# A two-layer model's MLPs: seven block products for the up matrix alone, or for the down matrix too

## What is computed

```python
        hn = rmsnorm(x, p['norm_mlp'][layer])
        u = jnp.maximum(hn @ p['w_up'][layer], 0)
        x = x + (u * u) @ p['w_down'][layer]
```

## Time and profile before

| what | value |
|---|---|
| median of 3 runs | 3455.08 us |
| lowest and highest | 3453.11 and 3457.73 us |
| span of the profiled execution (the page gives no other time for it) | 3458.2 us |
| PE busy | 3249.8 us, 94% |
| DVE, ACT, POOL busy | 1632.3, 1045.6, 1291.6 us |
| matmuls | 22572, of them 11568 at L2229 in the two MLPs |
| DMA | 205.13 MB, mean 59 GB/s |

### The profile page before, as it was taken

One profiled execution on the slowest core, in us unless ns is written; L12 is line 12 of the kernel. 1 busy time (PEld: TensorE's weight loads), 2 busy tenths in 40 slices (PEclk: granted clock), 3 DMA queues, 4 the chain that ended last, 5 costly groups with the idle time before them and its releaser, 6 DMA issues. The chain is left out here.

```text
span 3458.2 us, 54690 instructions
## 1 busy us (share of the span) xinstructions
PE 3249.8 (94%) x22572; PEld 3033.5 (88%) x22572; DVE 1632.3 (47%) x2715; ACT 1045.6 (30%) x1940; POOL 1291.6 (37%) x878
## 2 busy tenths in 40 slices
PE   7999988899999999999998898999889999999998
PEld 7999867889999999997887587788669999999998
DVE  5961157626544445541012254565564744455443
ACT  5310145324332232341001233233232422223334
POOL 4433224444644444454321121111124544444453
PEclk9999989999999999999999898999899999999999
DMA  4111323231111111123232322000231111111111
GB/s 146 43 38 56 102 26 73 47 104 44 43 50 43 38 50 50 50 70 130 78 102 72 89 44 59 9 6 8 93 137 42 45 44 37 50 50 50 50 38 71
DMA packets 257881, 205.13 MB, mean 59 GB/s; under 512 B 66053, under 2 KB 222207, under 8 KB 257220
## 3 DMA queue, kind: packets, MB, share of 16 engines
q1 hardware_dynamic: 252108, 201.21, 19.9%
q10 hardware_dynamic: 5528, 0.45, 0.1%
HBM read 159.42 MB, written 33.40 MB: 56 GB/s over the span
## 5 line engine op out<-in xcount | busy, mean ns | idle before, releaser
L2229 PE MATMUL ps<-u_r,wslots_r 128*128 128x272 f32 x5784 | 747.5, 289 | 9.3 <-DVE u_r L2565 3.0
L2229 PEld LDWEIGHTS ps<-u_r,wslots_r 128*128 128x128 f32 x5784 | 735.7, 189 | 14.7 <-DVE u_r L2565 6.1
L2229 PE MATMUL ps<-low_r,wslots_r 128*128 128x272 f32 x3312 | 579.3, 289 | 5.1 <-ACT low_r L2392 3.2
L2229 PEld LDWEIGHTS ps<-low_r,wslots_r 128*128 128x128 f32 x3312 | 479.2, 189 | 7.3 <-ACT low_r L2392 4.3
L2229 PE MATMUL ps<-hn_r,wslots_r 128*128 128x272 f32 x2472 | 476.3, 291 | 4.7 <-DVE hn_r L2565 3.0
L2575 DVE TENSOR_TENSOR xT<-xT,ps 128x544 f32<-128x544 f32 x480 | 338.4, 718 | 285.6 <-PE ps L2229 285.5
L2229 PEld LDWEIGHTS ps<-hn_r,wslots_r 128*128 128x128 f32 x2472 | 375.7, 190 | 8.1 <-DVE hn_r L2565 6.1
L2486 POOL TENSOR_TENSOR wslots<-rawm 128x512 f32<-128x512 f32 x150 | 197.6, 1318 | 379.4 <-PE ps L2229 367.6
L1777 PE MATMUL ps<-hn_r,wslots_r 128*128 128x364 f32 (+1 forms) x1392 | 274.6, 330 | 11.0 <-DVE Z L1990 4.9
L2491 POOL TENSOR_TENSOR wslots_r<-rawd,wslots_r 128x512 fp32r<-128x512 f32 x128 | 169.5, 1335 | 278.4 <-ACT wslots_r L2375 278.4
L1777 PEld LDWEIGHTS ps<-hn_r,wslots_r 128*128 128x128 f32 x1392 | 236.3, 189 | 17.5 <-DVE Z L1990 7.6
(11 more groups left out here) (705 smaller groups left out, 5662.2 us busy)
## 6 DMA issues: line engine op xcount, KB each, us to landing
rawm<-in_w_up SPq DMA_DIRECT2D x63, 512.0 KB, 4.7
rawd<-in_w_down SPq DMA_DIRECT2D x112, 256.0 KB, 2.8
raw<-in_w_in_even SPq DMA_DIRECT2D x28, 512.0 KB
xT<-x_saved SPq DMA_DIRECT2D x2, 4368.0 KB, 15.6
more_r<-more_r SPq DMA_DIRECT2D x28, 256.0 KB, 3.4
xT<-in_cache_fox_kv SPq DMA_DIRECT2D x12, 512.0 KB, 4.0
x_saved<-Z SPq DMA_DIRECT2D x1, 4368.0 KB, 14.8
Z<-in_x_prompt SPq DMA_DIRECT2D x8, 512.0 KB, 4.7
```

The source lines that it names most:

```text
L2229: m = pe.matmul(acc(i)[:, c], r32(w), r32(moved[:, qw * c:qw * (c + 1)]), start=start, stop=stop, skip_group_check=True)
```

## The change

`mlp_fourteen` replaces `mlp_seven`. It has two phases with seven block products in each.

**Upward.** Group 0 is plain as before; sets 1 to 15 are the seven products "1563724" of a group. The variant used has only 4 weight sums (`s1` to `s4`, two of them in place) and nests its results: a product accumulates onto the PSUM bank of an earlier one, once ACT has copied that (`first`) or DVE has added it (`more`). After the ReLU and the square, DVE makes four differences of the four hidden blocks (`differences`, `last_difference`), and SP stores all seven, squares and differences, as float32 to DRAM (`hid`).

**Downward.** 16 further sets, two for each 512 rows of `w_down`, again seven products "1563724" of 24 matmuls each (two output tiles x 12). The operand of a product is loaded back from DRAM over the place of the input block that is no longer needed, a pair of tiles at a time, rounded by ACT (`operand_high`) and reduced by DVE (`operand_low`). DVE adds each bank to the residual after each product (`added`), 14 times per set. The same four weight sums are made by POOL.

**Queues.** `raw` and a new `rawn` hold two sets of raw weights, loaded in four DMAs of 256 KB. SP's order per upward set is: weights of the set after next, then the seven stores. The final tiles of the residual come at eight points in the last two sets (`closes`) instead of one by one. Group 0's down product, which stood between the plain products and group 1, is gone from there.

The core of the diff:

```diff
-def mlp_seven(pr, I, layer, ps, W, wslots, rawd, xT, x, u, row, gx, norm, ending, saved=None):
+def mlp_fourteen(pr, I, layer, ps, W, wslots, rawn, hid, xT, x, u, row, gx, norm, ending, saved=None):
...
+    order, slot_of = "1563724", (0, 2, 1, 3)
+    top = G - 1
+    jobs = [(s, m) for s in range(1, 2 * G) for m in order]
...
+    closes = {(14, "3"): down[0:2], (14, "7"): down[2:4], (14, "2"): down[4:6], (14, "4"): down[6:8],
+              (15, "7"): down[8:12], (15, "2"): down[12:14], (15, "4"): down[14:16]}
+    adds_to = {"1": (0, 0), "5": (4, 1), "6": (0, 1), "3": (0, 1), "7": (4, 1), "2": (0, 0), "4": (4, 0)}
...
+    def turns(j):
+        s, x = 1 + j // 7, j % 7
+        y = j - 7 * (G - 2) - 3
+        found = [(0, order[y])] if 0 <= y < 7 else []
+        for q in range(1, Q):
+            y = j - 7 * (G - 1 + 2 * (q - 1)) - 6
+            if 0 <= y < 7:
+                found.append((q, order[y]))
+        return found
+    stores = [f"st_{n}" for n in ("h11", "h12", "h22", "h21", "t1", "t2", "t4")]
...
+            for s in range(1, top):
+                need(pool_, ("low", (s, "4")))
+                load_weights(s + 2)
+                for m in "3156724":
+                    store(s, m)
...
+            def up(s, m):
+                need(pool_, ("low", (s, m)))
+                if m == "1":
+                    need(dve_, ("hidden", s - 2, "h21") if s > 1 else ("hidden", 0, "h11"))
+                elif m == "5":
+                    need(dve_, ("more", s - 1, "h12") if s > 1 else ("hidden", 0, "h12"))
+                elif m == "2":
+                    need(dve_, ("more", s - 1, "h11") if s > 1 else ("hidden", 0, "h22"))
+                elif m in "637":
+                    need(act_, ("first", s, {"6": "h11", "3": "h22", "7": "h12"}[m]))
...
+            def room(d, m, i):
+                if m == "1":
+                    return ("added", d - 1, "2", i) if d else (("hidden", top - 1, "h21"), ("more", top, "h12"))[i]
+                if m == "5":
+                    return ("added", d - 1, "4", i) if d else (("more", top, "h11"), ("hidden", top, "h21"))[i]
+                return ("added", d, {"6": "1", "3": "5", "7": "6", "2": "3", "4": "7"}[m], i)
...
+            def first(s, m):
+                name = {"1": "h11", "5": "h22", "6": "h12"}[m]
+                need(pe_, ("M", s, m))
+                sem, value = parked_sem(name, s - 1)
+                act.wait_ge(s_[sem], value)
+                need(dve_, ("t3", s - 1))
+                step(("first", s, name), A.activation(two(park(name, s)), acc(up_acc(s, m)), ACT.Copy))
...
+            for j, (s, m) in enumerate(jobs):
+                if s < G and m in "156":
+                    first(s, m)
+                if j + 4 < len(jobs):
+                    high_of(jobs[j + 4])
+                if s < G and m in "3724":
+                    square(s, {"3": "h12", "7": "h22", "2": "h11", "4": "h21"}[m])
+                for q, mm in turns(j):
+                    operand_high(q, mm)
...
+            for s, m in jobs:
+                if m == "1":
+                    s1(s)
+                if m == "5":
+                    s3(s)
+                    s2(s)
+                if m == "6":
+                    s4(s)
+                low_of((s, m))
...
+            def differences(g):
+                need(act_, ("square", g, "h12"))
+                need(act_, ("square", g, "h11"))
+                parked_free("t1", g)
+                step(("t1", g), V.tensor_tensor(park("t1", g), park("h12", g), park("h11", g), ALU.subtract))
+                need(act_, ("square", g, "h22"))
+                need(dve_, ("t1", g))
+                parked_free("t2", g)
+                step(("t2", g), V.tensor_tensor(park("t2", g), park("h22", g), park("t1", g), ALU.subtract))
+                step(("t3", g), V.tensor_tensor(park("h12", g), park("h12", g), park("h22", g), ALU.subtract))
...
+            waiting = []
+            for j, (s, m) in enumerate(jobs):
+                d = s - G
+                if s < G:
+                    if m in "372":
+                        more(s, m)
+                    if m == "2":
+                        differences(s)
+                    if m == "4":
+                        need(pe_, ("M", s, "4"))
+                        parked_free("h21", s)
+                        need(dve_, ("t4", s - 1))
+                        hidden(s, "h21", acc(up_acc(s, "4")))
+                        last_difference(s)
+                else:
+                    added(d, m, 0)
+                    added(d, m, 1)
+                for q, mm in turns(j):
+                    operand_low(q, mm)
+                for n, t in waiting:
+                    lower(n, t)
+                waiting = closes.get((d, m), []) if low is not None else []
```

More of the change, by code:

```diff
@@ L2230, in product, with plain @@
                 return m
-            X = (XH, XL)
[L2232 to L2237, removed]
+            for i in range(NC + 1):
+                m = pe.matmul(sums[0:width[i], i:i + 1], norm["total"][:, P * i:P * i + width[i]], W["ones"][:, 0:1], start=True, stop=True)
+            done(m, "sums")
+            def plain(k, t):
+                return slice(TP * k + hw * t, TP * k + hw * t + hw)
+            X = (XH, XL)
             wa, wb = (wslots[:, 0], wslots[:, 2]), (wslots[:, 1], wslots[:, 3])
@@ L2387, in unit @@
[L2387 to L2399 removed]
+                step(("high", job), A.activation(r32(slot(job, 0)), source(job), ACT.Copy))
@@ L2460, in _ @@
-            for n, t in down:
-                c = slice(hw * t, hw * t + hw)
-                if (n, t) in ((2, 1), (4, 1)):
-                    high_of(("D", last - 1, 1 + n // 2))
-                    high_of(("D", last, 1 + n // 2))
-                need(dve_, ("add", G - 1, n, t))
-                step(("squared", n, t), A.activation((squares(n) if n else total)[:, c], xT[:, n, c], ACT.Square))
-                step(("scaled", n, t), A.activation(r32(high[:, n, c]) if rounded is not False else high[:, n, c], xT[:, n, c], ACT.Copy, scale=gcols[:, n:n + 1]))
+            high_of(jobs[0])
@@ new lines, in _ @@
+            for k in range(4):
+                x_high("6", k)
+            high_of(jobs[1])
+            square(0, "h12")
+            square(0, "h11")
+            for m in "47":
+                for k in range(4):
+                    x_high(m, k)
+            square(0, "h22")
+            high_of(jobs[2])
+            high_of(jobs[3])
+            square(0, "h21")
+            for j, (s, m) in enumerate(jobs):
[7 more added lines that the diff above has]
+                    operand_high(q, mm)
+                for n, t in closes.get((s - G, m), []):
+                    c = slice(hw * t, hw * t + hw)
+                    if n in (2, 3) and t:
+                        need(pe_, ("N", 15, "7", 1))
+                    need(dve_, ("final", n, t))
+                    step(("squared", n, t), A.activation((squares(n) if n else total)[:, c], xT[:, n, c], ACT.Square))
+                    step(("scaled", n, t), A.activation(r32(high[:, n, c]) if rounded is not False else high[:, n, c], xT[:, n, c], ACT.Copy, scale=gcols[:, n:n + 1]))
@@ new lines, in x_low, with hidden @@
+            def x_low(m, k):
+                hi, lo = operand(m, k)
+                need(act_, ("x_high", m, k))
+                if m == "6":
+                    need(dve_, ("x", "7", k))
+                    need(dve_, ("x", "4", k))
+                step(("x_low", m, k), V.tensor_tensor(r32(lo), lo, r32(hi), ALU.subtract))
+            def hidden(g, name, src):
+                t = 1 if name in ("h12", "h22") else 0
+                step(("hidden", g, name), V.scalar_tensor_tensor(out=two(park(name, g)), in0=src, scalar=0.0, in1=two(norm["row"][:, hw * t:hw * t + hw]),
+                                                                 op0=ALU.max, op1=ALU.mult))
@@ new lines, in more, with parked_free @@
+            def more(s, m):
+                name = {"3": "h12", "7": "h22", "2": "h11"}[m]
+                need(pe_, ("M", s, m))
+                need(act_, ("first", s, name))
+                t = two(park(name, s))
+                step(("more", s, name), V.tensor_tensor(t, t, acc(up_acc(s, m)), ALU.add))
+                need(dve_, ("more", s, name))
+                hidden(s, name, t)
+            def parked_free(name, g):
+                if g:
+                    sem, value = parked_sem(name, g - 1)
+                    dve.wait_ge(s_[sem], value)
@@ L2682, in _ @@
-            for y, (n, t) in enumerate(down):
-                add(G - 1, n, t)
-                if low is not None and y >= 1:
-                    lower(*down[y - 1])
-            if low is not None:
-                lower(*down[-1])
+                x_sum("4", k)
+            need(pe_, ("plain", 1, 1))
+            for k in range(4):
+                x_sum("7", k)
+            hidden(0, "h22", acc(2))
+            for k in range(4):
+                x_low("6", k)
```

(1 more changed line is left out.)

626 lines of the change are left out of this document (240 added, 386 removed).

## The result

The changed kernel takes 3513.84 us, the median of four runs (3512.21 to 3519.5), against 3454.61 for the kernel before in the same comparison: a ratio of 1.0169, interval 1.0155 to 1.0184, some 59 us slower. 3535 was forecast.

The account below looks back on a forecast made before the run. The prediction took the MLP to be bound by PE's rate. Savings of 48.5 us a layer against added waits, start, end and clock gave +40 a layer, +80 in both: 3455 + 80 = 3535 us, range 3392 to 3590.

Parts of the forecast that it names:

- 384 matmuls fewer: Downward part of each layer's MLP falls from 3072 to 2688 matmuls at 0.1264 us each: 48.5 us less a layer.
- waits at "6": Upward set borders: PE waits at product "6" for ACT's copy of "1", 14 times 2.4 us, 34 a layer, bounds 0 to 41.
- first downward set: Border from upward to downward phase: operand rounding and low parts delay PE by 6.1 + 2.5, 9 us a layer, bounds 3 to 12.
- downward pairs: Borders of downward sets: PE waits behind operand low parts and adds, 7 pairs x 2.3 = 16 us a layer, bounds 0 to 20.
- start: Start of each MLP: PE at 867 instead of 850.7, 16 less the 4.8 lost today: 11 us a layer, bounds 5 to 16.
- end: End of each MLP: POOL's 14 additions of squares finish later after PE, costing 7.5 and 6 us, together 13, bounds 0 to 20.
- clock, beyond the start: Half clock after PE's waits loses 1.7 us after one of two, 0.85 for each of 14: 12 us a layer, bounds 0 to 24.
- The chain: Upward borders: sums, squares and differences queue on POOL, ACT and DVE, so PE restarts near 15.0 instead of 12.1: 2.9 or 1.8 us.
- rival (2): Faster: DVE's three differences run without POOL between, so upward waits and clock loss vanish; 3405, or 3384 with downward waits hidden; chance 0.29.
- The turn: DVE and POOL, both waiting, alternate in 0.59 + 1.16 = 1.75 us, not the 2.01 of two whole instructions.
- rival (4): Each turn holds the other engine a whole instruction, 2.01 us; "6" waits 4.2; 3609, or 3585 without the clock; chance 0.08.
- DMAs: Seven stores per set and the operand loads on SP's queue stay hidden: 0 us charged.

Follow-up runs that it names:

- e3: Changed kernel plus one wait: POOL's fourth weight sum waits for DVE's third difference of the set before; 3457.16 us, ratio 1.0005 to the kernel before.
- e2: Changed kernel with ACT copying the next set's product 1 before squaring h21, waiting for the first difference only; 3430.52 us, ratio 0.9925 to the kernel before.
- e8: Changed kernel without activation stores and their waits, downward operands loaded from rows of the up weights instead; 3514.05 us, ratio 1.0166 to the kernel before.
- e7: e5 with differences reordered (set 0's earlier, later sets' behind h21's ReLU) and DVE adding one token half's squares; 3371.89 us, 0.9763 to the kernel before.
- e5: e2 plus, in the downward phase, ACT rounding the operand ahead of the weights' high part; 3396.83 us, ratio 0.9830 to the kernel before.

## Why the prediction was right

By its own steps, layer 0, predicted against measured:

| step | predicted us | measured us |
|---|---|---|
| 384 matmuls fewer | -48.5 | -48.5 (count as predicted) |
| waits at "6" | 34 | 36.4 |
| first downward set | 9 | 5.6 + 0.8 = 6.4 |
| downward pairs | 16 | 12.0 + 1.4 = 13.4 |
| start | 11 | 9.8 |
| end | 7.5 | 13.2 - 5.75 = 7.5 |
| clock, beyond the start | 12 | 6.0 + 3.5 = 9.5 |
| small waits of before, not credited | 0 | -6.1 |
| sum | 41 | 28 |

The last product of layer 0 ends 23.8 us later after its MLP's first matmul than before (773.3 against 749.5), and the gap behind it is 7.5 longer: 31.3. That is 3 us more than the measured terms give; 0.6 of it are two new waits of 0.3, and the rest I can't account for. Both layers together gave +59 where +80 was forecast.

**The chain** held in every link. It was written down that "6" would wait, on ACT's copy, 14 times a layer by 1.8 to 2.9 us, in sets of 23 to 24.1: measured 14 times 2.6, in 23.95. Of the two orders it left open, the one in which POOL's fourth sum is ahead of the first difference came, by 0.08 us. For it the chain gave 2.9, and 2.6 was measured; 2.4 was the middle of 2.9 and 1.8, so that 34 lies so near 36.4 is partly the luck of an average. The three moments of the differences were hit to 0.13 us, and e3 showed that it is the catching that makes them. The point that rival (2) named as decisive was indeed decisive: with the differences free of POOL the wait fell to 0.85 and the kernel to 3457.16. It did not fall to nothing, as the rival had it: in e3 the high part of POOL's delayed fourth sum and the square of h21 still stand in front of the copy. e2, where the copy stands ahead of that square and POOL's sum is not delayed, came to 3430.52.

**The turn** was taken as 1.75 us from rows of the kernel before. DVE's differences took 1.63 to 1.80, and POOL's parts between them 1.76. The Trainium skill, "SBUF — State Buffer", section "SBUF: two separate sides", has the two engines exclude each other for whole instructions. The runs agree that one waits out the other. But at 2.01 a turn (0.72 + 1.29) the copy would have been five times 0.26, or 1.3, later, and the wait 4.2 by the forecast's sum or 3.9 from the measured 2.6. The longest of the 14 was 2.6, and so rival (4) falls. Additions with one operand in PSUM stayed free, as forecast: 215 of them at L2614, between 1240 and 1580 us, took 0.70 to 0.72, with POOL busy 70% of that time.

**DMAs** at zero were right as far as stores go (e8). The 14.3 of that term is when the landing of h11's store is wanted, not when the store is asked for.

**The end** in layer 0 came at the forecast size: 14 additions of squares by POOL at 1.6 each, 22.4 us from about 10 us before PE's end. POOL's timeline of the changed kernel there:

```profile
1576.09 22.41 POOL L2531 TENSOR_TENSOR row<-row,low 128x544 f32<-128x544 f32 x14
```

DVE's, the low parts of the last tiles:

```profile
1591.90 7.19 DVE L2629 SCALAR_TENSOR_TENSOR xT_r<-xT,gcols,hn_r 128x544 fp32r<-128x544 f32 x4
```

PE's, the last product and the first work behind the MLP:

```profile
1583.63 3.18 PE L2292 MATMUL ps<-u_r,wslots_r 128*128 128x272 f32 x24
1600.03 2.27 PE L2872 MATMUL ps<-sb_ones,row 128*128 128x1 f32 x10 [13.23 <-PEq L76]
```

PE ended at 1586.8, POOL 11.7 and DVE 12.3 later (12.4 was predicted for POOL). So POOL was nearly as late as forecast, but DVE's low parts, which stood in no term, ended last; here the number is right partly by luck, and e7, which relieved POOL alone, gained only 3.0 in layer 0. In layer 1, which has no such low parts, the term was 7.7 against 6.

**What was mis-sized.** The step that failed is the small waits. Before, PE waited 9.2 us in layer 0, of which the start's 1.8 and 1.3 were credited; the other 6.1, waits of 0.2 at the borders of groups and one of 2.3 near the end among them, went too, and stood in no term. The first downward set (6.1 and 2.5 charged, 5.6 and 0.8 measured) and the pairs (16 charged, 13.4 measured) were charged for more waits than came. Together that is 11 us a layer; the waits at "6" came out 2.4 above their term, the start 1.2 and the clock 2.5 below theirs. One recorded sum is wrong but carries nothing: with the downward waits hidden, rival (2)'s own start and end give 3358 + 35 = 3393, not 3384.

**The clock** came out near in sum and wrong in kind. It was put behind one half of the 14 waits, at 1.7 us each. Windows that begin 2 us behind the restarts at 1179.85 and 1203.80, after waits of 2.60 and 2.61, show both outcomes; the third is the first downward set (PEclk is the third number from the end):

```profile
1181.80:1184.80 3.00, 3.00 (x26) 3.00 (x25) 0.00 (x0) 1.14 (x2) 1.47 (x2) 1.00 0.04 11
1205.90:1208.90 3.00, 3.00 (x15) 3.00 (x15) 0.00 (x0) 0.51 (x1) 0.89 (x1) 0.53 0.94 316
1231.50:1234.00 2.50, 2.50 (x12) 2.50 (x12) 1.73 (x2) 2.50 (x4) 0.45 (x1) 0.50 0.95 360
```

Only 4 of 14 waits of 2.6 us were followed by a stretch at 0.50 (1.2 GHz), of about 3.4 us each. Such a stretch loses 1.5 us, not half of its length: the restarts at 1033.14 and 1058.60, with one between them, lie 25.46 apart, and those without one 23.95. That makes 4 x 1.5 = 6.0 us where 12 were charged. In layer 1 it was 3 of 14. The DMA share (the last number but one), which differs so much in the first two windows, is not what tells them apart: the 3.5 us from 3103.39 on, behind such a wait, read 1.00 at a share of 0.92, and those from 2956.76 on read 0.57 at 0.00. The first downward set added 3.5 (132 matmuls from 1231.33 to 1252.13 took 20.15 us without the 0.65 of waiting, at 0.1264 each they take 16.7), which I had not charged. That the term is near is thus partly luck. e5 bounds it from another side: it removes some 97 us of waits in the two layers (135.5 to about 38, by the same view) and gains 117, so some 20 us went with the waits without being waits. PE's busy time bears out that they are the clock's: the same 10800 matmuls took 1702.1 us in e5, 24 less than in the changed kernel.

The start's 9.8 is made of the wait of 11.7 and 2.7 of half clock behind it, less 1.8, 1.3 and 1.5 that stood there before. The forecast that the MLP's PE time would fall "by some 97" was careless: it fell by 77, since a matmul at half clock is busy longer (the mean went from 289 to 292 ns), and the forecast had charged such stretches itself.

## What to carry to other kernels

When fewer matmuls are bought with work on the other engines, compare not their average loads but the longest chain between two products, each instruction put in its engine's queue in order; here loads of 66% (POOL) and 49% (DVE) in the window of one set still cost 2.6 us a set. Then look for the one instruction that PE waits for and ask which steps stand ahead of it without it needing them: two small edits of ACT's order (e5) turned 1.7% slower into 1.7% faster. And where DVE and POOL share a stretch, holding the one off the path back can be the gain.

## What the runs showed that was not expected

- A wait put in front of POOL made the kernel 57 us faster (e3), where 39 to 54 had been forecast.
- Waits of one length, 2.6 us, 23.95 us apart, were followed by the half clock 4 times in 14 and by full clock 10 times in layer 0, and 3 and 11 times in layer 1. Nothing that I read in the profile told the two apart; it stays open.
- Once the copy was early (e2, e5), the landing of a store became what released it, and in layer 1 it held PE up by 0.4 and 0.9 us. A trip that costs nothing in one order need not be free in a faster one.
